# Up projections of four feed-forward layers: one 512-wide product for a high weight block, halves summed on VectorE, a bank per half tile

## The reference

```
# layers 0 and 1
ffn = (silu(x @ w_ffn_gate[l]) * (x @ w_ffn_up[l])) @ w_ffn_down[l]      # 1024 -> 2816 -> 1024
x = layer_norm(ALPHA * x + ffn, ...)
# layers 2 and 3: the 5632 columns of x @ w_up are convolved over three tokens (taps of their own
# for every column), halved into value and gate, and silu(gate) * value goes through w_down
x = x + conv_ffn(rmsnorm(x), w_up, conv_w, conv_b, w_down)
```

## Time and profile before

| | |
|---|---|
| three runs, median (lowest to highest) | 1415.61 us (1413.43 to 1415.87) |
| span of the profiled execution, first to last instruction | 1411.6 us |
| TensorE matmul busy | 1359.9 us, 96% of the span, 10120 instructions |
| VectorE busy | 961.0 us, 68% |
| ScalarE busy | 729.6 us, 52% |
| GpSimd busy | 97.0 us, 7% |
| mean granted clock of TensorE | 0.991 of full speed |

### The profile page before, as it was taken

The page is one execution under the profiler, slowest core; times in us unless marked ns, Lnnn a source line. Parts: engine busy times, 40 slices in busy tenths (PEclk is TensorE's granted clock), DMA queues, the critical chain, the costliest instruction groups (busy, mean ns, idle before and its releaser), DMA issues.

```text
span 1411.6 us, 24784 instructions
## 1 busy us (share of the span) xinstructions
PE 1359.9 (96%) x10120; PEld 1249.6 (89%) x10120; DVE 961.0 (68%) x1624; ACT 729.6 (52%) x1216; POOL 97.0 (7%) x79
## 2 busy tenths in 40 slices
PE   9999899999999988999998999999999999999998
PEld 8997599999899767999988998889998998889997
DVE  5767775555859567655575786688778555687776
ACT  4855443334486644433345655554556555654554
POOL 0330000000005100000000011011110000000000
PEclk9999999999999999999999999999999999999999
DMA  8852255555453314655543434545554533545541
GB/s 317 290 184 69 90 179 180 182 183 187 152 194 120 133 54 145 236 179 179 182 150 134 157 113 147 180 140 193 193 192 166 194 115 126 194 171 187 180 179 60
DMA packets 38632, 233.24 MB, mean 165 GB/s; under 512 B 5016, under 2 KB 8808, under 8 KB 12152
## 3 DMA queue, kind: packets, MB, share of 16 engines
q1 hardware_dynamic: 36456, 224.18, 45.4%
q0 software_dynamic: 2064, 7.47, 1.7%
HBM read 230.55 MB, written 1.09 MB: 164 GB/s over the span
## 4 chain that ended last, share of the span: by engine, by line
PE 80%; DVE 11%; ACT 5%; issue 2%; DMA 1%; POOL 0%; DVEq 0%; SPq 0%; ACTq 0%
PE bank L776 19%; PE bank L777 19%; PE bank L778 19%; PE bank L784 4%; PE bank L785 4%; PE bank L788 4%; DVE w_lo L603 3%; PE bank L910 1%; ACT w_hi L593 1%; DVE arena L1770 1%; PE bank L1000 1%; PE bank L1035 1%; PE bank L1022 1%; DVE x L1719 1%; DVE res L1714 1%
## 5 line engine op out<-in xcount | busy, mean ns | idle before, releaser
L603 DVE TENSOR_TENSOR w_lo<-raw,w_hi 128x1024 fp32r<-128x1024 f32 x404 | 489.3, 1249 | 102.3 <-ACT w_hi L593 97.6
L776 PE MATMUL bank<-a_hi,w_hi 128*128 128x256 f32 x1856 | 529.9, 286 | 5.6 <-DVE w_lo L603 5.6
L777 PE MATMUL bank<-a_lo,w_hi 128*128 128x256 f32 x1856 | 526.3, 284 | 0.0
L778 PE MATMUL bank<-a_hi,w_lo 128*128 128x256 f32 x1856 | 526.1, 283 | 0.0
L593 ACT ACTIVATE w_hi<-raw 128x1024 fp32r<-128x1024 f32 x404 | 405.8, 1049 | 93.4 <-PE bank L778 62.4
L776 PEld LDWEIGHTS bank<-a_hi,w_hi 128*128 128x128 f32 x1856 | 357.0, 192 | 11.2 <-issue 8.3
L777 PEld LDWEIGHTS bank<-a_lo,w_hi 128*128 128x128 f32 x1856 | 357.1, 192 | 1.2
L778 PEld LDWEIGHTS bank<-a_hi,w_lo 128*128 128x128 f32 x1856 | 357.2, 192 | 0.0
L1770 DVE SCALAR_TENSOR_TENSOR arena<-bank,conv_col,arena 128x254 f32<-128x254 f32 (+1 forms) x176 | 76.6, 476 | 46.4 <-ACT arena L1328 44.8
L784 PE MATMUL bank<-w_hi,a_hi 128*128 128x256 f32 (+1 forms) x320 | 99.2, 331 | 7.4 <-ACT a_hi L1431 3.1
L777 PE MATMUL bank<-w_lo,h_hi 128*128 128x512 f32 x264 | 105.2, 399 | 0.0
(11 more groups left out here) (274 smaller groups left out, 1892.3 us busy)
## 6 DMA issues: line engine op xcount, KB each, us to landing
raw<-in_stream SPq DMA_DIRECT2D x201, 1024.0 KB, 4.9
bias_t<-bias_rows SPq DMA_DIRECT2D x6, 512.0 KB, 7.0
heads_buf<-in_w SPq DMA_DIRECT2D x2, 1024.0 KB, 8.7
gains<-in_w SPq DMA_DIRECT2D x2, 1024.0 KB, 10.7
gains<-in_ln_g POOLq DMA_DIRECT2D x4, 512.0 KB, 4.0
gains<-in_ln_b POOLq DMA_DIRECT2D x4, 512.0 KB, 5.8
gains<-in_rms_g POOLq DMA_DIRECT2D x3, 512.0 KB, 4.0
res<-in_xT SPq DMA_DIRECT2D x4, 256.0 KB, 5.0
```

What stands on the lines that cost most here:

```text
L603: dve.tensor_tensor(w_lo[:, i % PARTS, half_tile(h)], raw[:, i % SLOTS, half_tile(h)], w_hi[:, i % PARTS, half_tile(h)].bitcast(F32), ALU. ...
L776: pe.matmul(out, lh, rh, start=first, stop=False)
L777: pe.matmul(out, lh, rl, start=False, stop=False)
L778: return pe.matmul(out, ll, rh, start=False, stop=last)
```

## The change

`a_hi` and `a_lo` become the two parts of one tensor `a_both`, 8 KB apart. For up tiles of j >= 2 a new `channels_apart` uses one bank for each half tile c. Per block k it issues one matmul of 512 moving columns (the high weights against high and low rows at once; the results stand in the two halves of the bank) and one of 256 (the low weights against the high rows, added to the first half). ScalarE then copies the second half of the bank to SBUF (`part_low`), and VectorE adds the first half and that copy into `part_sum`, which ends the use of the bank. All that followed reads `part_sum` in SBUF in place of the bank. Up tiles 0 and 1 stay as they were.

```diff
-        uses += [((l, "up", j), "N") for j in [HEAD] + list(range(HEAD)) + list(range(HEAD + 1, FT))]
+        uses += [(key, "N") for j in [HEAD] + list(range(HEAD)) + list(range(HEAD + 1, FT)) for key in up_banks(l, j)]
+def up_banks(l, j):
+    return [(l, "up", j)] if j < HEAD else [(l, "up", j, c) for c in range(2)]
-        a_hi = sb("a_hi", [P, KT, S], F32R)
-        a_lo = sb("a_lo", [P, KT, S], F32R)
+        a_both = sb("a_both", [P, 2, KT, S], F32R)
+        a_hi, a_lo = a_both[:, 0, :, :], a_both[:, 1, :, :]
@@ TensorE
+            def channels_apart(b, key, c):
+                high, low = [part.rearrange("p (k c) -> p k c", k=KT)[:, :, c * P:(c + 1) * P]
+                             for part in weights(key)]
+                for k in range(KT):
+                    pe.matmul(b, high[:, k, :], a_both[:, :, k, :], start=k == 0, stop=False)
+                    mm = pe.matmul(b[:, 0:S], low[:, k, :], a_hi[:, k, :], start=False, stop=k == KT - 1)
+                return mm
-                            b = open_bank((l, "up", j))
-                            channels(b, (l, f"up{j}"), 0)
-                            close_bank(channels(b, (l, f"up{j}"), 1))
+                            for c, key in enumerate(up_banks(l, j)):
+                                close_bank(channels_apart(open_bank(key), (l, f"up{j}"), c))
@@ ScalarE
+            def up_part(l, j, c, summed=True):
+                if j < HEAD:
+                    return bank_of((l, "up", j))[:, c * S:(c + 1) * S]
+                key = up_banks(l, j)[c]
+                wait_full(act, key)
+                if j > HEAD:
+                    wait_drained(act, up_banks(l, j - 1)[c])
+                act.activation(part_low[c], bank_of(key)[:, S:2 * S], ACT.Copy).then_inc(low_copied, 1)
+                if summed:
+                    wait_drained(act, key)
+                return part_sum[c]
             def up(l, j):
-                wait_full(act, key)
                 if j >= 2:
                     act.wait_ge(h_done, l * FT + j - 1)
+                if j < HEAD:
+                    wait_full(act, (l, "up", j))
+                first = up_part(l, j, 0)
                 if l < 2:
-                    act.activation(gate_a[j % 2], b[:, 0:S], ACT.Silu).then_inc(act_gate, 1)
+                    act.activation(gate_a[j % 2], first, ACT.Silu).then_inc(act_gate, 1)
+                    up_part(l, j, 1, summed=False)
                 else:
-                    act.activation(cval[j % 2], b[:, 0:S], ACT.Identity, scale=..., bias=...)
-                    act.activation(cgate[j % 2], b[:, S:2 * S], ACT.Identity, ...).then_inc(conv_in, 1)
+                    act.activation(cval[j % 2], first, ACT.Identity, scale=..., bias=...)
+                    act.activation(cgate[j % 2], up_part(l, j, 1), ACT.Identity, ...).then_inc(conv_in, 1)
@@ VectorE
             def up(l, j):
+                    for c, key in enumerate(up_banks(l, j)):
+                        dve.wait_ge(low_copied, 2 * (l * (FT - HEAD) + j - HEAD) + c + 1)
+                        dve.tensor_tensor(part_sum[c], bank_of(key)[:, 0:S], part_low[c],
+                                          ALU.add).then_inc(*drained(key))
                 if l < 2:
                     dve.wait_ge(act_gate, l * FT + j + 1)
-                    dve.tensor_tensor(full, gate_a[j % 2], b[:, S:2 * S], ALU.mult).then_inc(*drained(key))
+                    step(dve.tensor_tensor(full, gate_a[j % 2], parts[1], ALU.mult))
                 else:
...
-                                c[:, lag:], b[:, i * S:(i + 1) * S - lag],
+                                c[:, lag:], parts[i][:, 0:S - lag],
...
-                    dve.nop().then_inc(*drained(key))
+                    if j < HEAD:
+                        dve.nop().then_inc(*drained(head))
```

More of the change, by code:

```diff
@@ L410, in build @@
         gain4 = arena[:, 5120:5120 + D]
+        part_low, part_sum = [[arena[:, at + c * S:at + (c + 1) * S] for c in range(2)] for at in (9856, 9856 + 2 * S)]
         used[0] = 0
@@ L489, in build @@
         act_gate = sem("act_gate")
+        low_copied = sem("low_copied")
         conv_in = sem("conv_in")
@@ L538, in wait_used @@
             elif kind == "up":
-                wait_full(eng, (l, "up" if number >= HEAD else "head", number))
+                wait_full(eng, (l, "up", number, 1) if number >= HEAD else (l, "head", number))
             else:
@@ L1314, in feed_forward @@
                         split_behind(act, (l, f"{kind}{j}"), split_high)
+            def up_part(l, j, c, summed=True):
[9 more added lines that the diff above has]
+                return part_sum[c]
             def up(l, j):
-                key = (l, "up", j)
-                wait_full(act, key)
-                b = bank_of(key)
                 if j >= 2:
                     act.wait_ge(h_done, l * FT + j - 1)
+                if j < HEAD:
+                    wait_full(act, (l, "up", j))
+                first = up_part(l, j, 0)
                 if l < 2:
-                    act.activation(gate_a[j % 2], b[:, 0:S], ACT.Silu).then_inc(act_gate, 1)
+                    act.activation(gate_a[j % 2], first, ACT.Silu).then_inc(act_gate, 1)
+                    up_part(l, j, 1, summed=False)
                 else:
                     m = l - 2
-                    act.activation(cval[j % 2], b[:, 0:S], ACT.Identity, scale=conv_col[:, m, j, 2:3],
+                    act.activation(cval[j % 2], first, ACT.Identity, scale=conv_col[:, m, j, 2:3],
                                    bias=conv_col[:, m, j, 3:4])
-                    act.activation(cgate[j % 2], b[:, S:2 * S], ACT.Identity, scale=conv_col[:, m, FT + j, 2:3],
+                    act.activation(cgate[j % 2], up_part(l, j, 1), ACT.Identity, scale=conv_col[:, m, FT + j, 2:3],
                                    bias=conv_col[:, m, FT + j, 3:4]).then_inc(conv_in, 1)
@@ L1755, in up @@
             def up(l, j):
-                key = (l, "up", j)
-                b = bank_of(key)
+                head = (l, "up", j)
                 full = h_full[j % 2]
+                if j < HEAD:
+                    parts = [bank_of(head)[:, c * S:(c + 1) * S] for c in range(2)]
+                else:
+                    parts = part_sum
+                    for c, key in enumerate(up_banks(l, j)):
+                        dve.wait_ge(low_copied, 2 * (l * (FT - HEAD) + j - HEAD) + c + 1)
+                        dve.tensor_tensor(part_sum[c], bank_of(key)[:, 0:S], part_low[c],
+                                          ALU.add).then_inc(*drained(key))
                 if l < 2:
                     dve.wait_ge(act_gate, l * FT + j + 1)
-                    dve.tensor_tensor(full, gate_a[j % 2], b[:, S:2 * S], ALU.mult).then_inc(*drained(key))
-                    wait_drained(dve, key)
+                    if j >= HEAD:
+                        wait_drained(dve, up_banks(l, j)[1])
+                    step(dve.tensor_tensor(full, gate_a[j % 2], parts[1], ALU.mult))
+                    if j < HEAD:
+                        dve.nop().then_inc(*drained(head))
                 else:
```

## The result

| | before | after |
|---|---|---|
| median of four runs (lowest to highest) | 1414.52 us (1412.65 to 1415.87) | 1481.94 us (1480.52 to 1482.27) |
| ratio after / before, 95% interval | | 1.0474 (1.0461 to 1.0486) |
| span of the profiled execution | 1411.6 us | 1480.3 us |
| mean granted clock of TensorE | 0.991 | 0.971 |

What follows compares the result with a forecast made beforehand. TensorE, 96% busy, bound the kernel; in layers 2 and 3 the ScalarE–VectorE loop would become the bound. Layers 0 to 3: +2.3, +4.0, +34.4, +25.6, together +66.3 on the 1411.6 us span; median 4.0 above, 1482 us, range 1460 to 1502.

Steps and rivals of the forecast that it cites:

- The serial steps ahead of the taps: Layers 2 and 3: sums, scalings and second copy pass between VectorE and ScalarE before the taps, 2.40 us per up tile.
- The loop against TensorE: Layers 2 and 3: the ScalarE–VectorE loop needs 18.61 us a round against TensorE's 16.88 and becomes the bound; layer 3 +25.6 us.
- GpSimd: Layer 2: its additions stretch pairs of weight splits by 0.55 us, no longer hidden; 16 of them make 8.8 us.
- The banks: Up tile 3 waits for up 2's first bank: +3.0 us layer 0, +4.7 layer 1; 8.1 in layers 2 and 3, no new cost.
- The clock behind the stops: Layers 0 and 1: TensorE runs at a slow clock after the stop ahead of up 3, 1.5 us each, bounds 0 to 2.
- Rival 3: TensorE's waits in the rounds bring slow clock stretches again and again: +10 to +25 us, about 1500; chance 0.09.
- The merged product: TensorE, up tiles: one 512-column matmul at 232.9 ns replaces two of 256 at 239.8; 0.11 us a tile, 8.8 for 80.
- the third stays: TensorE, up tiles: of three 256-column matmuls per block and half, the one not merged stays as before, at 119.9 ns.
- Rival 4: The merged matmul saves nothing, running like two matmuls; layers 0 and 1 lose their 4.4 us: 1486; 0.81 together with the forecast.
- The prediction's own sign of being wrong: A 512-column matmul starting under 227 or over 240 ns before the next would put TensorE's part wrong.
- Rival 1: First half's copy, sum and scale finish under TensorE's second half; 1.48 us ahead of the taps, +21, 1437 us; chance 0.07.
- Rival 2: TensorE stays the bound and the stops are hidden, so the kernel gets 8.8 us faster: 1407; chance 0.03.

Runs made afterwards that it cites:

- copies_first: The kernel after, with ScalarE copying the low halves of both banks before it scales (or takes silu); 1451.0 us.
- no_gpsimd: The kernel after, with 15 of GpSimd's 16 bias additions in layer 2 left out; 1472.4 us.
- heads_free: The kernel after, with up tiles 2 and 3 in the old form (one bank each, three matmuls per block); 1461.5 us.
- banks_only: The kernel after, keeping a bank per half tile but with the merged product, copies and sums taken back; 1444.1 us.
- merged_no_sum: banks_only plus the 512-wide matmul; the second half of the bank is left out of the result, no copies or sums; 1431.4 us.
- two_layers: The change in layers 0 and 1 alone, from up tile 4 on; layers 2 and 3 as in the kernel before; 1411.3 us, ratio 0.9979.
- before_plus_sums: The kernel before, with two unread VectorE additions of 256 columns for each up tile from 2 on; 1422.7 us.

## Why the prediction held

**The serial steps ahead of the taps (2.40 us, bounds 2.0 to 2.8): right.** 2.45 us were measured, and the even-to-odd step is 8.20 us for a forecast of 8.15. The scalings out of SBUF did take 0.04 us more, 0.60 for the 0.56 of the earlier trace rows. copies_first shows that this row of hand-overs is the cause: 31 of the 67 us went when two of its five steps were taken out of it.

**The loop against TensorE: right.** Rounds of 18.67 us for 18.61 in layer 3, 19.75 for 19.7 in layer 2; one wait of 1.65 us in a round for 1.7, behind `w_lo`; 26.5 us for 25.6 over layer 3, 34.3 for 34.4 over layer 2. The 0.9 us in layer 3 are 0.06 in each of seven rounds and 0.5 from the taps of tile 2 to those of tile 4 (18.88 for 18.39). Its last stretch answers to the earlier trace rows: from the taps of tile 21 to `h_hi` 4.57 us for 4.66.

```profile
1458.43 1.80 DVE L1811 SCALAR_TENSOR_TENSOR arena<-arena,conv_col 128x255 f32<-128x255 f32 x4 [0.67 <-ACT arena L1359]
...
1463.00 0.29 DVE L1826 TENSOR_SCALAR h_hi<-arena 128x256 fp32r<-128x256 f32 x1
```

**GpSimd (8.8 us in layer 2): right.** The part shrank by 7.7 us in the trace of no_gpsimd, for 15 of the 16, where 15 x 0.55 is 8.3.

**The banks (3.0 and 4.7 us; 8.1 in layers 2 and 3, at no cost): right.** 4.00 - 0.79 = 3.2 and 5.40 - 1.44 = 4.0 us. The 0.7 us that layer 1 lacks are the DMA, which landed 1.0 us earlier against the transposes than in the kernel before. The waits in layers 2 and 3 are 7.91, and heads_free shows that they cost nothing of their own in the kernel after.

**The clock behind the stops (1.5 each, bounds 0 to 2): too small in layer 1.** Up 3 took 7.29 - 5.61 = 1.7 us more in layer 0, and 8.51 - 5.61 = 2.9 in layer 1, outside the bounds. I had let the slow stretch be 4 us long at most, from the one in the earlier trace rows. A stop needs no 4.90 us for it either: 2.96 us were enough here. But the same stop does not always cost the same: in layer 0, waits of 2.96 to 3.02 us were followed by 0.1 us (banks_only), 1.7 (after) and 2.8 us (no_gpsimd) lost in up 3. A single price of 1.5 was within this range by chance.

**Rival 3, the clock in the rounds.** In the rounds of layer 3 it stayed up, 1.00 from 1290 to 1440. In layer 2 it did fall: from 945 to 1130 the granted clock was 0.94. That cost nothing, since VectorE's rounds there are all 19.74 to 19.77 us; TensorE waits for it in any case. So the mechanism of rival 3 exists in layer 2, but not its price.

**The merged product (0.11 us a tile, 8.8 us): mis-sized.** The 232.9 ns, taken from the down tile, held: over the 18 full-clock up tiles of a layer a 512 takes 233.5 ns in the mean. The step that failed is "the third stays". The 256 behind a 512 takes 117 ns, where the forecast kept the 119.9 of a 256 among others. A pair of both takes 347 ns in some rounds (230 and 117) and 353 in others (236 and 117 in the mean), 350.5 over all, for the 352.8 forecast. So an up tile takes 5.61 us in place of 5.75, 0.145 us saved, 11.6 us over 80 tiles for the 8.8; merged_no_sum bears that out behind up 3. Rival 4 is dead. The prediction's own sign of being wrong, a 512 over 240 ns, does occur: in the slower rounds one 512 in three takes 241. The mean is what counts in the sum. In layers 0 and 1 the term is 2.9 us a layer for the 2.2 forecast.

**The sum is better than its terms.** Layer 0: 3.2 + 1.7 - 2.9 = 2.0 (measured 2.0) for a forecast of 2.3. Layer 1: 4.0 + 2.9 - 2.9 = 4.0 (4.0) for 4.0. In layer 1 the forecast had the stop 0.7 us too long, the gain of the product 0.7 too small and the slow clock 1.4 too cheap, and these cancelled. Over the four parts the forecast of 66.3 met 66.9, by the reading of the loop.

That the median was hit within 0.1 us is luck on top. I took the median of the runs to lie 4.0 us above the profiled span, since the profiled execution before was the shortest of its three; after, it lies 1.6 above. This made up for the 2.4 us by which the forecast of the span, 1477.9, was short of 1480.3.

**The other rivals.** Rival 1, the first half out of the way, supposed 1.48 us a tile. The kernel after doesn't do it, for the reason given: sum 0 starts when VectorE comes to it, and that is late. copies_first measures nearly its price, 1.58 us. Rival 2 is false for the whole kernel, but its mechanism is real in layers 0 and 1, where two_layers gains 3.4 us in the median.

## What to carry to other kernels

When two engines hand a tile to and fro in fixed order, list what each has in its queue and add up the steps that can only begin when the slower engine arrives. Set that sum against the idle time per round; the busy shares of the page (68% and 52% here) say nothing about it. If such steps must be added, put first in each queue what waits for no one: taking one copy out of the row was worth 31 us.

A change that takes twice the buffers per item costs at the point where another use stands between two items (the transposed heads here), and nowhere else in the loop; look there, and try the first items in the old form (20.5 us here). A saving on the engine that is the bound counts only in those stages where it stays the bound.

Where two kernels differ by a few us in a part that no edit touched, look first at what each engine waited for ahead of it. A DMA that landed 2.5 us later against TensorE moved up tile 3 of layer 1 by as much (banks_only against merged_no_sum).

## What the runs showed of the hardware

- A moving operand in two stretches of 256 columns, 8 KB apart, costs nothing beyond the 512 of the down tile: 233.5 ns from start to start in the mean, nearly all between 230 and 241, against 232.9. Against the 227 ns of the output projection it is 6 ns more, and no run here tells if that is the two stretches.
- A 256 that follows a 512 takes 117 ns, one among other 256s 119.9.
- The spacing of the same stream of matmuls has two values, 347 and 353 ns a pair, that take turns from round to round; among the four up tiles without a down tile between them (18 to 21) it does not change. The program doesn't fix which comes first: with the same list for TensorE, layer 0 of no_gpsimd has them the other way round than that of the kernel after. I tried nothing on the cause, and it stays open.
- The clock fell to 1.2 GHz behind stops of 2.45 us (before_plus_sums, layer 1) and 2.96 us (after, layer 0), and stayed at 2.4 GHz behind one of 3.02 us (banks_only, layer 0). Up tile 3 lost 1.7 and 2.9 us behind stops of 2.96 and 4.36 us.
- Two neighbouring copies on ScalarE overlap: 0.64 us for both in copies_first, where one takes 0.36.

```profile
1373.43 0.64 ACT L1340 ACTIVATE arena<-bank 128x256 f32<-128x256 f32 x2
```

The Trainium skill (ScalarE: Activation LUTs, section What ACT_TABLE_LOAD costs) gives about 93 ns for this overlap. The trace agrees, with 2 x 0.36 - 0.64 = 0.08 us. In the kernel after only the copy behind scale 0 gets it, 0.60 us long and followed by the copy after 0.51.
